# Compression inputs read from PSUM, first rows ahead of the next pair's logits, gated outputs split around the last weighted values

## What is computed

```python
def compress_blocks(t, pe, w1, w2):
    nc = (S - CMP_BLOCK) // CMP_STRIDE + 1
    idx = jnp.arange(nc)[:, None] * CMP_STRIDE + jnp.arange(CMP_BLOCK)[None, :]
    blk = t[:, :, idx] + pe
    flat = blk.reshape(B, G, nc, CMP_BLOCK * dh)
    return jax.nn.silu(flat @ w1) @ w2
...
kc = compress_blocks(kv_heads(kc_raw, NSA_KV_HEADS), pe_cmp_k[l], w_cmp_k1[l], w_cmp_k2[l])
vc = compress_blocks(kv_heads(vc_raw, NSA_KV_HEADS), pe_cmp_v[l], w_cmp_v1[l], w_cmp_v2[l])
...
o_a = gts[0] * o_cmp + gts[1] * o_slc + gts[2] * o_win
y_a = (merge_heads(o_a) * jax.nn.silu(z_a)) @ w_o_nsa[l]
y_b = (merge_heads(o_b) * jax.nn.silu(z_b)) @ w_o_swa[l]
y = (jax.nn.sigmoid(m_a) * y_a + jax.nn.sigmoid(m_b) * y_b) @ w_out[l]
```

## Time and profile before

| | us |
|---|---|
| median of three runs | 1572.1 |
| lowest and highest | 1568.7 and 1576.1 |
| the profiled execution, its own time | 1576.7 |
| its span in the trace | 1575.0 |

### The profile page before, as it was taken

The page is one execution under the profiler, slowest core; times in us unless marked ns, Lnnn a source line. Parts: engine busy times, 40 slices in busy tenths (PEclk is TensorE's granted clock), DMA queues, the critical chain, the costliest instruction groups (busy, mean ns, idle before and its releaser), DMA issues.

```text
span 1575.0 us, 24782 instructions
## 1 busy us (share of the span) xinstructions
PE 1505.0 (96%) x9498; PEld 1352.1 (86%) x9498; DVE 747.3 (47%) x1555; ACT 529.6 (34%) x944; POOL 597.2 (38%) x481
## 2 busy tenths in 40 slices
PE   3999999999999899999999999999999999999996
PEld 2678888888877899999999999988888879879885
DVE  6846656566657843233233231233623552362364
ACT  4444334343423522322322322333322332341332
POOL 5562222222154344444443544433343353343321
PEclk9999999998999899999999999999999999999997
DMA  9232111111225123222222222222132132213111
GB/s 375 95 119 81 55 53 53 53 53 30 104 81 214 54 81 108 80 80 107 80 80 107 80 84 104 80 68 87 61 107 85 62 107 80 88 58 107 56 52 54
DMA packets 23635, 140.28 MB, mean 89 GB/s; under 512 B 3352, under 2 KB 3352, under 8 KB 7712
## 3 DMA queue, kind: packets, MB, share of 16 engines
q1 hardware_dynamic: 18320, 127.93, 22.7%
q10 hardware_dynamic: 5264, 11.64, 2.2%
HBM read 137.45 MB, written 2.11 MB: 89 GB/s over the span
## 4 chain that ended last, share of the span: by engine, by line
issue 42%; PE 29%; POOL 23%; DVE 4%; ACT 1%; DMA 1%; POOLq 0%; DVEq 0%; ACTq 0%
PE lin L388 24%; POOL w_lo L329 22%; PE aux L925 3%; PE aux L897 1%; DMA residual<-x_t 1%; DVE mix L1782 1%; DVE square_sum L414 1%; PE aux L450 0%; POOL residual L361 0%; PE aux L906 0%; DVE squares L1800 0%; PE aux L422 0%; DVE tmp L1721 0%; DVE residual L1837 0%; DVE v_T L1778 0%
## 5 line engine op out<-in xcount | busy, mean ns | idle before, releaser
L329 POOL TENSOR_TENSOR w_lo<-w_raw,w_hi 128x512 fp32r<-128x512 f32 x448 | 583.6, 1334 | 945.2 <-ACT w_hi L376 945.2
L388 PE MATMUL lin<-x_hi,w_hi 128*128 128x512 f32 (+2 forms) x2056 | 558.8, 326 | 20.5 <-DVE x_lo L1323 6.9
L388 PE MATMUL lin<-x_lo,w_hi 128*128 128x512 f32 (+2 forms) x2056 | 552.4, 323 | 0.0
L388 PE MATMUL lin<-x_hi,w_lo 128*128 128x512 f32 (+2 forms) x2056 | 551.9, 323 | 0.0
L388 PEld LDWEIGHTS lin<-x_hi,w_hi 128*128 128x128 f32 x2056 | 343.6, 190 | 53.5 <-issue 11.4
L388 PEld LDWEIGHTS lin<-x_hi,w_lo 128*128 128x128 f32 x2056 | 342.2, 190 | 30.4
L388 PEld LDWEIGHTS lin<-x_lo,w_hi 128*128 128x128 f32 x2056 | 342.1, 190 | 26.5
L376 ACT ACTIVATE w_hi<-w_raw 128x1024 fp32r<-128x1024 f32 x224 | 223.7, 1048 | 148.2 <-PE lin L388 143.8
L1041 ACT ACTIVATE prob<-prob,neg_max 128x31 f32<-128x31 f32 (+6 forms) x128 | 60.2, 471 | 132.8 <-DVE neg_max L1450 132.8
L1588 DVE TENSOR_TENSOR conv_in<-conv_c_gate,lin 128x272 f32<-128x272 f32 (+1 forms) x30 | 11.6, 427 | 189.4 <-PE lin L388 189.4
L388 PE MATMUL lin<-mix,w_hi 128*128 128x512 f32 x256 | 81.9, 401 | 2.5 <-DVE mix L1782 1.9
(11 more groups left out here) (328 smaller groups left out, 1912.6 us busy)
## 6 DMA issues: line engine op xcount, KB each, us to landing
w_raw<-wstream SPq DMA_DIRECT2D x112, 1024.0 KB, 4.8
ada_shift_scale<-w_ada SPq DMA_DIRECT2D x8, 1024.0 KB, 20.7
ada_gate<-w_ada_gate ACTq DMA_DIRECT2D x4, 1024.0 KB, 5.3
residual<-x_t SPq DMA_DIRECT2D x1, 2048.0 KB, 10.4
residual<-x_t ACTq DMA_DIRECT2D x1, 2048.0 KB, 8.5
out_t<-residual ACTq DMA_DIRECT2D x8, 256.0 KB, 2.1
neg_m<-row_store ACTq DMA_DIRECT2D x4, 256.0 KB, 3.3
e_m<-row_store ACTq DMA_DIRECT2D x4, 256.0 KB, 3.3
```

The source lines that it names most:

```text
L329: eng.tensor_tensor(wlo[h][:, cols], raw[h][:, cols], whi[h][:, cols].bitcast(F32), ALU.subtract).then_inc(s_lo, 1)
L388: ins = t.matmul(o, w[half][:, c0:c0 + P], x(k, t0, cnt), start=(n == 0), stop=(n == 3 * kts - 1))
```

## The change

Three places are edited.

- `cmp_kv` and `copy_out(0)` go. `compression_input(src)` reads the PSUM bank of chunk 0 directly. TensorE, which overwrites these banks in `project(3)` and in `turn_values(0)`, waits for the inputs made from them instead of for the copies.
- In a pair that is not the last, three of the eight rows of the next pair's first tile (`ROWS_AHEAD`) stand ahead of the next pair's first logits, with a wait for the low part of the first of the two query tiles, whose bank they write. The other five stay where all eight were.
- Behind the last pair ScalarE makes six high parts before it waits for the last weighted values and issues the two loads. VectorE makes the first two low parts (`OG_AHEAD`) ahead of its wait for the last weighted values and a third behind the last outputs, ahead of their turning. TensorE begins with the rows of `w_o` at once, and turns the last outputs behind the second.

```diff
-        cmp_kv = sb("cmp_kv", [2, T1], stack=stage_c_right, side="right")
...
-        CREDIT = 2
+        CREDIT, ROWS_AHEAD, OG_AHEAD = 2, 3, 2
...
                     elif c == 3:
                         if g:
                             eng.wait_ge(s_gate_th, 1)
-                        eng.wait_ge(s_proj_out, g + 1)
+                        else:
+                            eng.wait_ge(s_cin, 1)
...
             def turn_values(s):
-                eng.wait_ge(s_proj_out, (4, 6, 8)[s])
+                eng.wait_ge(s_proj_out, (2, 4, 6)[s])
+                if s == 0:
+                    eng.wait_ge(s_cin, 2)
...
                     elif not last:
+                        eng.wait_ge(s_q, ii * 2 + 3)
+                        fill(ii + 1, FILL[False], 0, 0, slice(0, ROWS_AHEAD))
                         scores(0, ii + 1)
...
                 if not last:
-                    fill(ii + 1, FILL[False], 0, 0)
-                turn_outputs(QT - 1)
+                    fill(ii + 1, FILL[False], 0, 0, slice(ROWS_AHEAD, None))
+                    turn_outputs(ii, QT - 1)
...
             for n, k in enumerate(OG_ORDER):
+                if n == OG_AHEAD:
+                    turn_outputs(NPAIR - 1, QT - 1)
                 eng.wait_ge(s_og_lo, n + 1)
...
-            for c in range(2):
-                eng.wait_ge(s_pv, 8 * NPAIR)
-                eng.dma_start(gate_w[:, c, :], w_ada_gate[c, :, :]).then_inc(s_ada[c], 16)
             eng.wait_ge(s_chunk, START["wo"])
-            for k in OG_ORDER:
+            for n, k in enumerate(OG_ORDER):
+                if n == KD - 2:
+                    eng.wait_ge(s_pv, 8 * NPAIR)
+                    for c in range(2):
+                        eng.dma_start(gate_w[:, c, :], w_ada_gate[c, :, :]).then_inc(s_ada[c], 16)
...
-                eng.wait_ge(s_proj_out, 2)
+                    eng.wait_ge(s_chunk, START["proj"] + 1)
+                else:
+                    eng.wait_ge(s_proj, 1)
                 for g in range(2):
                     gs = slice(g * DH, (g + 1) * DH)
-                    rows_of = cmp_kv[gs, src, :].rearrange("p (j a r) -> p r a j", a=8, r=2)
+                    rows_of = proj_bank(0, src)[gs, :].rearrange("p (j a r) -> p r a j", a=8, r=2)
...
-            copy_out(0)
             compression_input(0)
...
+                    if s == 7 and last:
+                        eng.wait_ge(s_oT_out, 4 * (NPAIR - 1) + CREDIT)
+                        for k in range(OG_AHEAD):
+                            low_og(k)
                     eng.wait_ge(s_pv, ii * 8 + (s + 1))
...
+                if last:
+                    low_og(OG_AHEAD)
                 outputs_turned(QT - 1)
...
-            for k in range(KD):
+            for k in range(OG_AHEAD + 1, KD):
                 low_og(k)
```

## The result

The kernel after takes **1549.35 us**, the median of four runs from 1548.93 to 1550.01. The kernel before took 1572.93 in four runs beside it (1568.74 to 1576.07). The ratio is 0.985, with an interval from 0.982 to 0.988: 1.5% faster. The forecast of 1549 holds. The profiled execution took 1549.52, its span is 1547.8.

What follows compares the result with a forecast made beforehand. TensorE, busy 96% of the span, was taken as the bound. Gains of 4.5 + 5.1 + 12.0 + 3.9 = 25.5 us gave 1551.2 from the profiled execution, 1546.6 from the median; the middle, 1549 us, was forecast, range 1543.5 to 1560.

Steps and rivals of the forecast that it cites:

- 4.5 summed: Compression: TensorE's pauses of 3.02 and 1.50 us go, a gain of 4.5 us in all.
- The lower bound: Compression additions: 0.57 us each, as with GpSimd idle, chosen over the other bound of 1.38 beside GpSimd's work.
- The reason given for 0.57: Compression additions: the new form has operands like VectorE's PSUM passes, 0.70 us each, and half their length.
- bounded at 62.6: Compression: low part, both operands in SBUF beside GpSimd's pieces, ends between 61.4 and 62.6 us.
- 17.1 summed: Three pair turns: 5.1 us of pauses and 12.0 us of clock come back.
- The step that chose all of 12.0: Pair turns: without the pause the clock stays high, as in a pair's other steps; 12.0 us, other end 0.
- Rival 2: Pair turns: clock falls anyway, small matmuls still side by side; 1561 us at all turns, about 1557 at two; chance 0.12.
- The cover of 0.8 us for the exponentials: Pair turns: exponentials end at 198.5 us, TensorE needs them at 199.3; rival that this breaks, 1565 to 1570, chance 0.04.
- 3.9 summed: Behind the last pair: pauses of 1.2 and 1.4 us go, plus 1.3 us of clock.
- as the step said: Behind the last pair: TensorE ends the weighted values at 426.5 us and starts w_o rows at once.
- the middle: Whole kernel: 1549 us, between 1551.2 from the profiled execution and 1546.6 from the median.
- The guess behind it: Whole kernel: part of the profiled execution's 4.6 us above the median may be a longer low stretch of the clock.

Runs made afterwards that it cites:

- 4.4 alone: Kernel before with only the compression inputs read from their banks and the copies dropped: 1568.33 us against 1572.69, ratio 0.9975.
- the kernels that separate pause and small matmuls: Changed kernel with the three rows ahead of the turning of the last probabilities: 1553.04 us; with them behind the next pair's logits: 1556.0 us.
- the other parts present: Kernel before with compression inputs from banks and three rows ahead, without split outputs: 1553.76 us, set against the changed kernel's 1549.35 and 1548.57.
- the kernel with the third part alone: Kernel before with only the gated outputs split around the last weighted values: 1563.63 us, ratio 0.9948.
- the kernel with the second part alone: Kernel before with only three rows of the next pair ahead of its logits: 1558.48 us, ratio 0.9923.
- the one with ScalarE's copies: Kernel before, with ScalarE instead of VectorE copying the two banks into SBUF; additions keep both operands in SBUF: 1571.63 us, ratio 1.0.
- one and eight: Changed kernel with one row ahead of the next pair's logits instead of three: 1556.81 us; with all eight: 1556.72 us.
- the repetition: The changed kernel unaltered, measured again on another occasion: 1548.57 us, from 1546.3 to 1553.42, ratio 0.9846.

## Why the prediction was right, point by point

**Compression: 4.5 summed, 5.1 at its place, 4.4 alone.** The additions were taken at 0.57 us each and took 0.38. The lower bound was no bound: 0.57 was measured with both operands in SBUF, and the form with one in PSUM is faster still. The reason given for 0.57, a pass with a PSUM operand and half its length, points to half of 0.70, 0.35, which is nearer. It made no difference to the first set, because ScalarE's splitting of weights ended later either way, and gave the second keys 3.3 us to spare instead of 2.9 (76.1 against 79.4). The collision of the low part with GpSimd was foreseen, bounded at 62.6, and ended at 61.6; TensorE's first compression matmul came at 62.2, without a wait. 0.17 us of the 5.07 were there when VectorE began. The 3.0 us of pause was charged without the fall of the clock that can stand behind it; two of the four traces with this pause have one, of 1.7 us.

**Pair turns: 17.1 summed, 16.8 at the place.** The pauses (5.1) went, and all of the clock (12.0) came back. The step that chose all of 12.0 rested on an analogy with the other steps of a pair; the kernels that separate pause and small matmuls now carry it: without a pause of more than 0.5 us no fall, with one falls at most turns. Rival 2 has fallen for this order of work. The cover of 0.8 us for the exponentials, the thinnest, held at all three turns. The new wait of 0.36 us stands one step further on, at the second step of the last pair, which the prediction had not looked at; it accounts for the 0.3 by which the sum was high.

**Split outputs: 3.9 summed, 4.1 at the place, 4.4 to 5.2 by the medians with the other parts present.** Both pauses and the fall went; the first row of w_o starts 0.42 us after the last group of weighted values starts, as the step said.

**The frame.** The sum of 25.5 was to lie between the median and the profiled execution, and the middle was taken. By the medians 23.6 came, by the two spans 27.2. The guess behind it was that the profiled execution had spent more time at the low clock than a median one. The clocks on record bear it out: 0.981 in the profiled execution, 0.983 to 0.985 in the runs of the kernel before between 1572.2 and 1572.9 us. By estimate that is 3 to 6 us of full speed, and the 4.6 lies in it. Against this execution the change got back all 12.0 at the turns, and 3.4 more in stages that it leaves alone. That the middle met the median within 0.4 us is partly luck: the middle had no reason of its own, and such falls move a run by up to 7 us.

**The rule on idle gaps.** The prediction set the compression's 3.02 us, with no fall behind it, against the turns' 1.51 us with one. That contrast belonged to one execution. The same pause of 3.0 us stands in three more traces: no fall in the kernel with the third part alone, one of 1.7 us in the kernel with the second part alone and in the one with ScalarE's copies. So such a pause can be followed by a fall as well, in two traces of four, where the turns' 1.51 us was in 11 cases of 12. Idle time alone still doesn't order the cases: 0.8 us among small matmuls was followed by falls of 3.4 us at two turns of three, 3.0 us in the compression by none or one of 1.7. What exactly the chip weighs stays open, and so does why the same code falls in one execution and not in another (the kernel with ScalarE's copies had its 1.5 us pause at all three turns, and the clock fell only at the second and the third).

## What to carry to other kernels

Look at the granted clock around every pause of TensorE that stands among small matmuls: here 4.5 us of pauses in the waits table hid 12 us of lower clock, and moving nine large matmuls into each pause brought back both. Look at more than one execution before a pause is called harmless. When work is moved into a gap, ask what it covered where it stood; three rows ahead and five behind beat one and eight. And weigh an edit by what moved at its place in the trace: by place the three parts added up to within 0.2 us, while the medians of single parts differed from their places by up to 5.

## What the hardware showed

- An addition of 64x248 with a step of 16 elements takes 411 ns with one operand in PSUM, from 568 on with both in SBUF and GpSimd idle, and 1456 with both in SBUF beside GpSimd (medians, but for the 568). The strided read of a PSUM bank cost nothing that can be seen.
- GpSimd pays its share: its pieces take 1.45 us beside additions from SBUF and 1.26 otherwise. One piece met the low part of 128x992 and took 2.25, and the low part took 1.77 instead of 1.19.
- A pause of 0.8 us of TensorE between small matmuls was followed by 3.4 us lost at 1.2 GHz at two turns of three. One of 3.0 us between matmuls of 512 and 256 columns was followed by none in two traces (one of them) and by 1.7 us lost in two others.
- Falls in untouched stages vary between kernels and executions. In the traces of before and after they differ by 3.4 us of full speed, and the six runs of the repetition spread over 7 us, the slowest with the lowest mean clock.
